# Rotary's exchange of head halves: a permutation product on TensorE, or four DMAs between SBUF buffers

## What is computed

```python
def apply_rope(x, cos, sin):
    xf = x.astype(jnp.float32)
    x1, x2 = jnp.split(xf, 2, axis=-1)
    out = jnp.concatenate([x1 * cos - x2 * sin, x2 * cos + x1 * sin], axis=-1)
    return out.astype(x.dtype)

    q = apply_rope(q.reshape(b, s, 2, N_DIFF_HEADS, DIFF_HEAD_DIM), cos, sin)
    k = apply_rope(k.reshape(b, s, 2, N_DIFF_HEADS, DIFF_HEAD_DIM), cos, sin)
    v = v.reshape(b, s, N_DIFF_HEADS, DIFF_V_DIM)
    o = diff_attention(q, k, v, lam)
```

## Time and profile before

| what | value |
|---|---|
| median of three runs | 2479.69 us (2476.96 to 2483.39) |
| profiled execution, its own time | 2473.95 us |
| its span | 2472.3 us |
| TensorE busy | 2425.7 us, 98% |
| VectorE, ScalarE, GpSimd busy | 41%, 38%, 48% |

### The profile page before, as it was taken

One profiled execution on the slowest core, in us unless ns is written; L12 is line 12 of the kernel. 1 busy time (PEld: TensorE's weight loads), 2 busy tenths in 40 slices (PEclk: granted clock), 3 DMA queues, 4 the chain that ended last, 5 costly groups with the idle time before them and its releaser, 6 DMA issues.

```text
span 2472.3 us, 35533 instructions
## 1 busy us (share of the span) xinstructions
PE 2425.7 (98%) x14295; PEld 2004.9 (81%) x14295; DVE 1007.0 (41%) x2261; ACT 935.4 (38%) x1435; POOL 1182.7 (48%) x1566
## 2 busy tenths in 40 slices
PE   8999999999999999999999999999999999999998
PEld 6888888888788888888888888877868887888887
DVE  7974211124874211123867774224345333211113
ACT  5553222224563322224544453235553344322221
POOL 5125655654115565655533233443326645655563
PEclk9999999999999999999999999999999999999999
DMA  5532223224632223224211111232213322223222
GB/s 177 139 103 86 102 88 109 99 77 130 164 103 86 103 81 115 85 85 141 94 58 53 53 52 53 81 133 86 69 58 128 116 96 79 96 86 110 103 80 83
DMA packets 42403, 237.17 MB, mean 96 GB/s; under 512 B 4736, under 2 KB 7936, under 8 KB 19712
## 3 DMA queue, kind: packets, MB, share of 16 engines
q1 hardware_dynamic: 39936, 218.13, 25.0%
q0 software_dynamic: 2304, 16.78, 3.3%
HBM read 213.92 MB, written 4.19 MB: 88 GB/s over the span
## 4 chain that ended last, share of the span: by engine, by line
PE 91%; DVE 4%; POOL 2%; issue 1%; ACT 1%; DMA 1%; SPq 0%; DVEq 0%; POOLq 0%; ACTq 0%
PE PB L1886 75%; PE PB L1888 4%; POOL WL L3028 1%; PE PB L1898 1%; PE PB L1923 1%; PE PB L2136 1%; PE PB L2117 1%; DVE cc L2614 1%; PE PB L1970 1%; PE PB L1987 1%; PE PB L2124 1%; DMA WR<-in_w_in 1%; PE PB L2148 1%; PE PB L2164 1%; PE PB L2087 0%
## 5 line engine op out<-in xcount | busy, mean ns | idle before, releaser
L3028 POOL TENSOR_TENSOR WL<-WR,WH 128x256 fp32r<-128x256 f32 (+1 forms) x1444 | 1055.0, 767 | 753.6 <-ACT WH L2183 753.6
L1886 PE MATMUL PB<-HH,WH 128*128 128x512 f32 x1992 | 795.0, 399 | 11.0 <-ACT HH L2198 10.5
L1886 PE MATMUL PB<-HL,WH 128*128 128x512 f32 x1992 | 779.4, 391 | 0.9 <-DVE HL L2506 0.9
L1886 PE MATMUL PB<-HH,WL 128*128 128x512 f32 x1992 | 516.5, 396 | 0.8 <-DMA WL<-WR 0.8
L2183 ACT ACTIVATE WH<-WR 128x2048 fp32r<-128x2048 f32 (+1 forms) x209 | 371.9, 1779 | 245.9 <-PE PB L1886 238.2
L1886 PEld LDWEIGHTS PB<-HH,WH 128*128 128x128 f32 x1992 | 375.8, 189 | 101.2 <-issue 13.7
L1886 PEld LDWEIGHTS PB<-HL,WH 128*128 128x128 f32 x1992 | 375.8, 189 | 76.9 <-issue 1.7
L1886 PEld LDWEIGHTS PB<-HH,WL 128*128 128x128 f32 x1992 | 366.4, 188 | 75.3 <-issue 2.0
L1886 PE MATMUL PB<-BL,WH 128*128 128x512 f32 (+1 forms) x859 | 331.6, 387 | 0.6 <-DVE BL L2515 0.6
L1886 PE MATMUL PB<-BH,WH 128*128 128x512 f32 (+1 forms) x795 | 307.9, 388 | 1.3 <-ACT BH L2218 1.3
L1886 PE MATMUL PB<-BH,WL 128*128 128x512 f32 (+1 forms) x795 | 195.0, 389 | 1.5 <-POOL WL L3028 1.5
(11 more groups left out here) (363 smaller groups left out, 2678.4 us busy)
## 6 DMA issues: line engine op xcount, KB each, us to landing
WR<-in_w_gu SPq DMA_DIRECT2D x66, 1024.0 KB, 4.7
WR<-in_w_dn SPq DMA_DIRECT2D x48, 704.0 KB, 4.0
WR<-in_w_in SPq DMA_DIRECT2D x22, 1024.0 KB, 4.8
WL<-WR POOLq DMA_DIRECT2D x16, 1024.0 KB, 6.9
WR<-in_qkv SPq DMA_DIRECT2D x12, 1024.0 KB, 4.7
WR<-in_w_out SPq DMA_DIRECT2D x8, 1024.0 KB, 4.7
WR<-in_qk SPq DMA_DIRECT2D x8, 1024.0 KB, 4.8
WR<-in_gb SPq DMA_DIRECT2D x4, 1024.0 KB, 4.7
```

What stands on the lines that cost most here:

```text
L1886: ins = pe.matmul(out[:, 0:n], wt[:, k * cols + j * P:k * cols + (j + 1) * P], x[:, k, t0:t0 + n], start=first, stop=last)
L3028: g.tensor_tensor(m.WL[u % 2][:, part], m.WR[u % 2][:, part], f32(m.WH[u % 2][:, part]), ALU.subtract).then_inc(sems["wlo"], 1)
```

## The change

The four rows of the exchange are moved by DMA instead of a product. ScalarE waits for its own copy into qr, and for the buffer qs, and issues four DMAs, each from 32 partitions of qr to the 32 partitions that change place with them in one of three buffers qs. The product, its bank of PSUM and the constant C_SWAP are gone. VectorE multiplies qs by sine in place and adds it. A rotation is put into the order two tiles after its `qkin` instead of one, behind the beginning of the next unit. The table of costs changes with it: "rot" loses 0.9 us of TensorE and 0.1 of VectorE, "swap" has 0.4 us of ScalarE, and the planner takes a landing 5 us after `qkin`. Three semaphores are new, and the constants in SBUF shrink from 1736 to 1608 columns, by which the buffers behind them move.

```diff
-C_ID, C_ONE, C_INVF, C_SGN, C_SWAP, C_CAUS, ... = 0, 128, 256, 257, 264, 392, ...
+C_ID, C_ONE, C_INVF, C_SGN, C_CAUS, ... = 0, 128, 256, 257, 264, ...
...
+    names += [(f"qs{i}", [P, S]) for i in range(3)]
+    m.qs = pa[8:11]
...
-    "rot": [("T", 0.9, 0), ("V", 1.5, 0)],
+    "swap": [("A", 0.4, 0)], "rot": [("V", 1.4, 0)],
...
-        def rotate(name, c, q):
-            room = fbank.take()
-            t = Tile(room, room.after)
-            pe("rot", l, name, c, tile=t, q=q.i, tok=at("qkin", l, name, c), after=f)
-            room.free(at("rots", l, name, c))
+        def rotate(name, c, q, x):
+            step("rot", l, name, c, q=q.i, x=x.i, swapped=swapped[name, c], after=f)
             q.free(at("rot", l, name, c))
+            x.free(at("rot", l, name, c))
...
                     step("qkin", l, name, c, tile=t, q=q.i, after=q.after + rope)
                     room.free(at("qkin", l, name, c))
-                    if waiting:
-                        rotate(*waiting)
-                    waiting = name, c, q
+                    if len(waiting) == 2:
+                        rotate(*waiting.pop(0))
+                    x = qss.take()
+                    swaps[x.i] += 1
+                    swapped[name, c] = f"swap{x.i}", 64 * swaps[x.i]
+                    step("swap", l, name, c, q=q.i, x=x.i, after=x.after)
+                    clock.when[swapped[name, c]] = clock.when[at("qkin", l, name, c)] + 5.0
+                    waiting.append((name, c, q, x))
                     yield
...
                 room.free(at("vin", l, p, b))
                 if waiting:
-                    rotate(*waiting)
-                    waiting = None
+                    rotate(*waiting.pop(0))
...
-        elif kind == "rot":
-            te.all(w["tile"].after)
-            te.wait_ge(*at("qkin", *key))
-            pe.matmul(PB[w["tile"].b][:], m.CON[:, C_SWAP:C_SWAP + P], m.qr[w["q"]][:], start=True, stop=True).then_inc(tile, 1)
...
+        elif kind == "swap":
+            l, name, c = key
+            ae.wait_ge(*at("qkin", *key))
+            ae.all(w["after"])
+            for x in range(4):
+                a.dma_start(m.qs[w["x"]][32 * x:32 * x + 32, :], m.qr[w["q"]][32 * (x ^ 1):32 * (x ^ 1) + 32, :]).then_inc(sems[f"swap{w['x']}"], 16)
...
-            q, dst = m.qr[w["q"]], (m.Q if name == "q" else m.K)
-            ve.wait_ge(*w["tile"].done)
+            x, dst = m.qs[w["x"]], (m.Q if name == "q" else m.K)
+            ve.wait_ge(*w["swapped"])
             ve.wait_ge(*at("rsin", l))
+            v.tensor_tensor(x[:], x[:], m.RSIN[:], ALU.mult).then_inc(sems["rots"], 1)
+            ve.wait_ge(*at("rots", *key))
             ve.wait_ge(*at("rotc", *key))
-            v.tensor_tensor(q[:], PB[w["tile"].b][:], m.RSIN[:], ALU.mult).then_inc(sems["rots"], 1)
-            ve.wait_ge(*at("rots", *key))
-            v.tensor_tensor(dst[:, c, :], dst[:, c, :], q[:], ALU.add).then_inc(sems["rot"], 1)
+            v.tensor_tensor(dst[:, c, :], dst[:, c, :], x[:], ALU.add).then_inc(sems["rot"], 1)
```

More of the change, by code:

```diff
@@ L61 @@
 NVEC = _n
-C_ID, C_ONE, C_INVF, C_SGN, C_SWAP, C_CAUS, C_INCL, C_LEV, C_EYE, C_RST = 0, 128, 256, 257, 264, 392, 904, 1032, 1192, 1224
-NCON = 1736
+C_ID, C_ONE, C_INVF, C_SGN, C_CAUS, C_INCL, C_LEV, C_EYE, C_RST = 0, 128, 256, 257, 264, 776, 904, 1064, 1096
+NCON = 1608
 def constants():
@@ L73, in constants @@
     c[:, C_ONE:C_ONE + P] = 1.0
-    c[:, C_SWAP:C_SWAP + P] = (r ^ 32) == k
     c[:, C_CAUS + 384:C_CAUS + S] = np.where(k <= r, 0.0, NEG)
@@ L149, in memory @@
              ("cp0", [P, 30 + S]), ("cp1", [P, 30 + S]), ("cc0", [P, S]), ("cc1", [P, S]), ("ct", [P, S]), ("sm", [P, 96]), ("rcos", [P, S])]
-    names += [(f"pa{i}{n}", [P, S]) for i in range(3) for n in range(2)]
+    names += [(f"pa{i}{n}", [P, S]) for i in range(3) for n in range(2)] + [(f"qs{i}", [P, S]) for i in range(3)]
     m.qr0, m.qr1, m.Q, m.K, m.VT, m.cx, cp0, cp1, cc0, cc1, m.ct, m.sm, rcos, *pa = run(g1, b0, *names)
-    pa += run(tail1, end, ("pa30", [P, S]), ("pa31", [P, S]))
+    pa[6:6] = run(tail1, end, ("pa30", [P, S]), ("pa31", [P, S]))
+    m.qs = pa[8:11]
     m.RCOS, m.RSIN, m.R2 = rcos, m.ct, rcos
@@ L241 @@
     "lnsum": (), "lnsub": ("V:lnsub",), "lnmul": ("V:lnmul",), "lnact": ("A:lnact",),
-    "scaled": ("V:rcos", "V:rsin"), "r2": ("A:r2",), "qkin": ("A:qkin",), "rot": ("G:rotc", "V:rots", "V:rot"), "vin": ("A:vin",),
+    "scaled": ("V:rcos", "V:rsin"), "r2": ("A:r2",), "qkin": ("A:qkin",), "swap": (), "rot": ("G:rotc", "V:rots", "V:rot"), "vin": ("A:vin",),
     "sh1": ("V:sh1",), "sh2": ("V:sh2",), "sh3": ("V:sh3",), "sh4": ("V:sh4a", "V:sh4"),
@@ L873, in ffn @@
         return toks, fo2
-    rope = []
+    rope, swaps = [], [0, 0, 0]
     def block1(l, fo, then):
@@ L885, in block1 @@
         qrs = Ring([Room(i) for i in range(4)], clock)
-        for q in qrs.rooms:
+        qss, swapped = Ring([Room(i) for i in range(3)], clock), {}
+        for q in qrs.rooms + qss.rooms:
             q.free(*f)
@@ L942, in conv_taps @@
                 yield
-        turned = {}
-        def rotate(name, c, q):
-            room = fbank.take()
-            t = Tile(room, room.after)
-            pe("rot", l, name, c, tile=t, q=q.i, tok=at("qkin", l, name, c), after=f)
-            room.free(at("rots", l, name, c))
+        def rotate(name, c, q, x):
+            step("rot", l, name, c, q=q.i, x=x.i, swapped=swapped[name, c], after=f)
             q.free(at("rot", l, name, c))
-            turned[name, c] = True
+            x.free(at("rot", l, name, c))
         v_in = set()
         def heads_in(p):
-            waiting = None
+            waiting = []
             for name in "qk":
@@ L3069, in sync_program @@
     q.dma_start(m.VECS[:, 0:first_vecs], d["vecs"][:, 0:first_vecs]).then_inc(sems["vec0"], 16)
-    q.dma_start(m.CON[:, C_INVF:C_SWAP], d["con"][:, C_INVF:C_SWAP]).then_inc(sems["rope"], 16)
+    q.dma_start(m.CON[:, C_INVF:C_CAUS], d["con"][:, C_INVF:C_CAUS]).then_inc(sems["rope"], 16)
     q.dma_start(m.POSI[:], d["pos"]).then_inc(sems["pos"], 16)
@@ L3077, in sync_program @@
     q.dma_start(m.VECS[:, first_vecs:NVEC], d["vecs"][:, first_vecs:NVEC]).then_inc(sems["vec1"], 16)
-    q.dma_start(m.CON[:, C_SWAP:NCON], d["con"][:, C_SWAP:NCON]).then_inc(sems["con1"], 16)
+    q.dma_start(m.CON[:, C_CAUS:NCON], d["con"][:, C_CAUS:NCON]).then_inc(sems["con1"], 16)
     stored = 0
@@ L3113, in build @@
         o = order(m)
-        names = ["tile", "vchain", "vec0", "vec1", "con0", "con1", "rope", "pos", "w0", "w1", "wlo0", "wlo1", "memt", "away", "out"]
+        names = ["swap0", "swap1", "swap2", "tile", "vchain", "vec0", "vec1", "con0", "con1", "rope", "pos", "w0", "w1", "wlo0", "wlo1", "memt", "away", "out"]
         names += [f"x{c}" for c in range(DC)] + [f"bt{i}{j}" for i in range(2) for j in range(2)]
```

## The result

The median of five runs is 2506.05 us (2501.95 to 2508.59), against 2478.89 for the kernel before: a ratio of 1.0114 [1.0102, 1.0127], 28 us slower (brackets behind a ratio hold its 95% interval). The forecast was 2474.8 with a range of 2466 to 2488. The profiled execution took 2501.95 us with a span of 2500.6, 28.3 more than the span of before.

The account below looks back on a forecast made before the run. TensorE, busy for 98% of the span, was taken as the bound. Gains of 3.0 (layer 0) and 3.5 (layer 1) minus 1.6 for ScalarE gave 4.9 us less: 2469.0 profiled, 2474.8 as median, range 2466 to 2488.

Parts of the forecast that it names:

- Moved: Rotations in the first stage of both layers: VectorE's two instructions stay and come one tile later; counted at nothing.
- The rest of ScalarE's time: Second head pair: eight exchanges ahead of score-chain copies and exponentials cost 0.2 us each, 1.6 in all, within 0 to 12.8.
- cheap issue: Rival, chance 0.30: ScalarE's issue is short and the exchange does not slow weight copies; 10.1 us less, 2469.6.
- ScalarE late: Rival, chance 0.15: issues of 0.7 us or more delay value units and the second head pair's score chain; 2490.6 us.
- Removed: TensorE, first stage of both layers: 16 products of 0.87 us go, giving 13.9 us at most.
- Layers 0 and 1: Weight copies at key and value units: products ahead of waits give nothing, copies land later; net gains 3.0 and 3.5 us.
- Exchange late: Rival, chance 0.08: exchanges land after 9 us, VectorE loses 3 us at four places; 1 us less, 2478.8.
- A freed bank: The PSUM bank each product held comes free; TensorE has next to no idle time to fill, so counted at nothing.

Follow-up runs that it names:

- old order without products: Kernel before with its own costs and order, the 16 products left out and VectorE multiplying unexchanged qr by sine: 0.9967 of before, median 2470.33 us.
- new order without exchange: Kernel after in its own order, the 64 DMAs left out and VectorE multiplying unexchanged qr by sine: 1.0059 of the kernel before, median 2489.62 us.
- Either half of the edit alone: Before's kernel without products or exchange, only the planner's rotation cost on TensorE dropped, or only rotations deferred to two tiles: 1.0070 and 1.0069 of before.
- old order with ScalarE's exchange: Kernel before in its own order, products left out, four DMAs issued by ScalarE right behind each copy into qr: 1.0031 of before, median 2485.69 us.
- split ahead of the exchange: Kernel after, ScalarE splitting the next unit's weights before it issues the second tile's exchange, TensorE's order kept: 1.0084 of the kernel before, median 2495.51 us.

## Why the prediction was wrong

The measured parts, each from a pair of kernels. The third column is the difference of their ratios, times 2479 us (each uncertain by 3 to 5 us); the fourth is the difference of the two layers' stretches, from one profile of each kernel, and agrees:

| part | pair | us, by ratios | us, in the layers |
|---|---|---|---|
| products away, old order | before, old order without products | -8.2 | -6.8 |
| the new order | old and new order without exchange | +22.8 | +23.8 |
| ScalarE's exchange | new order without exchange, after | +13.6 | +15.5 |
| sum | before, after | +28.2 | +32.5 |

**The step that failed is "Moved"**: "The two VectorE instructions of a rotation stay ... and come one tile later in the order ... Counted at nothing." It asked who waits for a rotation within the stage, and that answer held: VectorE waited 0.8 us for an exchange, and nothing on TensorE waited for a rotation. It did not ask what the planner does with the edit. The rotation's place and its 0.9 us of TensorE are inputs of a program that lays out all the work of a layer, and its output changed up to 100 us behind the edit. The diff showed that the table of costs changes and that the rotation moves; no term of the sum and none of the rivals had a price for it, and the runs showed 22.8 us in place of the nothing. The list of what would prove the prediction wrong ended with "a changed order that moves the waits to another place altogether", with no price and no chance. Either half of the edit alone cost as much as the whole.

**The second failed step is "The rest of ScalarE's time", the term 1.6.** The idle share of 40% put it near the low end of 0 to 12.8. All that the sum charges for the exchange is 5.2 us (10.1 of *cheap issue* less 4.9); ScalarE's exchange cost 13.6 us in the new order and 16 in the old. In the layers' stretches 6.9 of its 15.5 us lie ahead of the first value tile, where the sum has 3.6, and 8.7 behind it, where the sum has this 1.6. Two sizes were off. The issue took 0.61 us and up to 1.65 instead of 0.41; an exchange is 2.4 to 4.3 us instead of 1.6. And the idle share said nothing of the moments at which ScalarE was wanted: in two later exchanges ScalarE ran nothing else for 3.4 and 3.2 us ahead of a copy and an exponential of the score chain (timeline of ScalarE, kernel after):

```profile
87.26 3.33 ACTq L2258 DMA_DIRECT2D qs<-qr  x4
90.64 0.55 ACT L2282 ACTIVATE pa<-PB 128x256 f32<-128x256 f32 x2 [3.41 <-issue]
...
106.43 3.13 ACTq L2258 DMA_DIRECT2D qs<-qr  x4
109.60 0.72 ACT L2275 ACTIVATE pa<-pa,sm 128x512 f32<-128x512 f32 x1 [3.21 <-issue]
```

In layer 0 TensorE's passes waited three times, 3.7 us together, for the copies of line 2282; in the new order without exchange they waited for none of them. Of the rivals, *ScalarE late* had this mechanism, with 0.15, and nearly its price: 11 us above before, where the old order with ScalarE's exchange stands 7.7 above. With its "0.7 us or more" it was also near the issue time. The kernel after is slower, as this rival says, but mostly for a reason that it does not have.

**Removed** held in kind. 13.9 us were the ceiling, and the products ahead of a waited-for copy gave nothing: 8.2 us came out with no issue at all, where *cheap issue* had worked out 10.1. By layer, the four stretches gave 0.6 us in layer 0 (4.3 expected with no issue ahead of the split) and 6.2 in layer 1 (5.8 expected). In layer 0 the wait for the copy is followed by 3.4 us at half clock, where before had none (1.7 us lost), and TensorE waits 1.9 us more in the score chain: 4.3 - 1.7 - 1.9 = 0.7.

**Layers 0 and 1**, the copies, came out in their numbers. Counted from the layer's first query copy, the value unit's low part started 1.1 us later than before in layer 0 (1.3 forecast) and 1.0 later in layer 1 (0.8 forecast); the waits of 4.1 and 3.4 us are about the "2 to 4" of the forecast, and the key unit waited 1.4 us. In layer 0 this was luck. The forecast moves the landing by as much as the issue, 10.0 us behind it. Without the exchange the copy was issued at 53.40 and landed 12.3 us later, and the low part started at 65.70, so 3.3 us of earlier issue were worth 0.6 us of earlier start at most. What holds the landing there stays open.

***Exchange late*** fell: landings of 1.9 / 2.6 / 7.5 us hurt nobody by more than 0.8 us. The Trainium skill ("DMA: Bandwidth & Descriptors", section "Rules for kernel authors") has disjoint partitions serialize. The trace doesn't bear out the estimate of 8.6 us that the prediction made of it, each piece waiting for the one before: four that were issued 0.6 us apart landed 2.6 us after issue in the median, and the DMA of 64 partitions took 3.3. Whether the pieces share the DMA engines can't be read from this. The Trainium skill's 50 ns for a dispatch (section "Anatomy of one DMA", given there for GpSimd's path), which would have made the change cheap, meets a shortest issue row of 514 ns on ScalarE.

**A freed bank** was counted at nothing. No run freed it alone, so its worth stays open.

## What to carry to other kernels

Where a planner writes the order, a change of a step's cost or place is a change of the whole order: make the old order without the step first, and compare, before pricing the step. An issue between SBUF buffers cost its queue about 0.6 us here, for 64 KB and for 128 KB alike, so count pieces, not bytes, and let a queue issue them whose next work is not waited for; a mean idle share does not show that ScalarE is such a queue. And a transfer that lands 10 us after its issue need not land earlier when it is issued earlier.

## What the runs showed of the hardware

- Issuing one DMA between SBUF buffers held the issuing queue for 0.51 us at least, 0.61 in the median and up to 1.65 on ScalarE, and 0.51 / 0.59 / 1.98 on SP, for 64 KB; 0.47 / 0.56 / 1.43 on ScalarE for 128 KB. In the kernel before, SP's issues of weight loads (line 3066) took 0.33 to 0.45 and those of 256 KB 0.33 to 0.71. Four in a row held ScalarE for 2.44 to 4.26 us.
- TensorE fell to a granted clock of 0.5 (the 1.2 GHz level) for 10.2 us in the output product, right behind a wait of 3.3 us and shorter ones. In the kernel before the layers had no such piece, and 10.2 us at that level are 5.1 us more for the same work.
- The value unit's weight copy of layer 0 (1 MB, GpSimd) did not land earlier for being issued earlier: issued at 56.69 it took 9.6 us (after), at 53.68 13.0 (split ahead of the exchange), at 53.40 12.3 with no exchange at all, and at 54.33 10.0. So the exchange is not the main cause, and the cause is open.
- Four exchange pieces of 64 KB, issued 0.6 us apart by ScalarE, landed 1.9 / 2.6 / 7.5 us after issue (minimum, median, maximum).
